# Attention in two chunks, and head work moved off GpSimd, in a decoder step on one core

## What is computed

```python
def step(carry, inp):                      # chunks of tokens, in order
    C, n, m = carry
    qc, kc, vc, li, lf = inp
    bcum = jnp.cumsum(lf, axis=-1)
    D = bcum[..., :, None] - bcum[..., None, :] + li[..., None, :]
    D = jnp.where(causal, D, -jnp.inf)
    inter = bcum + m[..., None]
    m_t = jnp.maximum(inter, jnp.max(D, axis=-1))
    s = jnp.einsum('bhjd,bhsd->bhjs', qc, kc) * jnp.exp(D - m_t[..., None])
    num = (jnp.einsum('bhjs,bhsd->bhjd', s, vc)
           + jnp.exp(inter - m_t)[..., None] * jnp.einsum('bhvk,bhjk->bhjv', C, qc))
    nq = jnp.sum(s, axis=-1) + jnp.exp(inter - m_t) * jnp.einsum('bhk,bhjk->bhj', n, qc)
    h = num / jnp.maximum(jnp.abs(nq), jnp.exp(-m_t))[..., None]
    w_s, decay = jnp.exp(bcum[..., -1:] - bcum + li - m_new[..., None]), ...
    C_new = decay[..., None, None] * C + jnp.einsum('bhs,bhsv,bhsk->bhvk', w_s, vc, kc)
```

## Time and profile before

| | us |
|---|---|
| median of three runs | 942.03 |
| lowest and highest | 940.66, 942.45 |
| span of the profiled execution | 940.7 |

### The profile page before, as it was taken

The page is one execution under the profiler, slowest core; times in us unless marked ns, Lnnn a source line. Parts: engine busy times, 40 slices in busy tenths (PEclk is TensorE's granted clock), DMA queues, the critical chain, the costliest instruction groups (busy, mean ns, idle before and its releaser), DMA issues. The chain is left out here.

```text
span 940.7 us, 18449 instructions
## 1 busy us (share of the span) xinstructions
PE 928.3 (99%) x6833; PEld 907.8 (96%) x6833; DVE 772.2 (82%) x1231; ACT 464.4 (49%) x684; POOL 106.7 (11%) x110
## 2 busy tenths in 40 slices
PE   8999999999999999999999999999999999999996
PEld 8999999999999999999999999999999999999995
DVE  6899985988698869876455569999888999889997
ACT  6654452445336324634833345456545555455664
POOL 3011330042006001500231000000000000000001
PEclk9999999999999999999999999999999999999998
DMA  6245216211620352042342222233222223232122
GB/s 219 68 150 198 69 57 224 90 45 56 246 90 23 134 191 90 23 150 87 117 140 68 89 73 84 90 108 106 102 90 91 90 68 113 90 116 109 46 91 100
DMA packets 22460, 98.56 MB, mean 105 GB/s; under 512 B 2929, under 2 KB 5122, under 8 KB 17909
## 3 DMA queue, kind: packets, MB, share of 16 engines
q1 hardware_dynamic: 19576, 77.13, 24.9%
q0 software_dynamic: 1984, 19.72, 5.7%
q10 hardware_dynamic: 832, 0.88, 0.3%
HBM read 85.28 MB, written 12.44 MB: 104 GB/s over the span
## 5 line engine op out<-in xcount | busy, mean ns | idle before, releaser
L1301 PE MATMUL ps<-h_hi,w_hi 128*128 128x288 f32 x896 | 193.7, 298 | 0.0
L1301 PE MATMUL ps<-h_lo,w_hi 128*128 128x288 f32 x896 | 191.7, 295 | 0.0
L1301 PE MATMUL ps<-h_hi,w_lo 128*128 128x288 f32 x896 | 191.4, 295 | 0.0
L793 ACT ACTIVATE w_hi<-raw 128x1024 fp32r<-128x1024 f32 x76 | 80.4, 1058 | 177.4 <-PE ps L1301 174.2
L1301 PEld LDWEIGHTS ps<-h_hi,w_hi 128*128 128x128 f32 x896 | 143.5, 189 | 1.3 <-issue 0.6
L1301 PEld LDWEIGHTS ps<-h_hi,w_lo 128*128 128x128 f32 x896 | 144.3, 189 | 0.0
L1301 PEld LDWEIGHTS ps<-h_lo,w_hi 128*128 128x128 f32 x896 | 144.2, 188 | 0.0
L1692 DVE TENSOR_TENSOR w_lo<-raw,w_hi 128x1024 fp32r<-128x1024 f32 x76 | 94.2, 1240 | 48.9 <-ACT w_hi L793 48.8
L1917 DVE SCALAR_TENSOR_TENSOR conv<-a_p,vec,conv x120 | 97.6, 813 | 0.2
L1569 PE MATMUL ps<-cols_b,late 128*128 128x288 f32 x432 | 62.8, 295 | 0.1
L1569 PE MATMUL ps<-cols_a,main 128*128 128x288 f32 x432 | 62.9, 295 | 0.0
(11 more groups left out here) (362 smaller groups left out, 1857.3 us busy)
## 6 DMA issues: line engine op xcount, KB each, us to landing
raw<-w_head_in SPq DMA_DIRECT2D x40, 512.0 KB, 3.5
raw<-w_fp_in SPq DMA_DIRECT2D x18, 1024.0 KB, 4.9
cs<-st_c_in POOLq DMA_DIRECT2D x4, 2048.0 KB, 9.6
c_s_out<-cs POOLq DMA_DIRECT2D x4, 2048.0 KB, 7.7
raw<-w_fo_in SPq DMA_DIRECT2D x8, 1024.0 KB, 4.9
x<-xT_in SPq DMA_DIRECT2D x16, 288.0 KB, 4.1
raw<-w_cgcv_in SPq DMA_DIRECT2D x8, 512.0 KB, 3.6
raw<-w_ga_in SPq DMA_DIRECT2D x8, 512.0 KB, 3.5
```

The source lines that it names most:

```text
L793: act.activation(w_hi[:, s, :], raw[:, s, :], ACT.Copy).then_inc(hi_ready, 1)
L1301: last = pe.matmul(ps[:, 2 * s + b, 0:HALF], wt[:, w, k * P:k * P + P], src[:, k, b * HALF:b * HALF + HALF], start=(k == 0 and wt is w_hi ...
```

## The change

S and PV are computed in two chunks of 256 prompt tokens. S0 and S1 end at column 256 (`S_END`). For the second chunk PV adds the weighted queries (`qt`, split into `qt_hi` by ACT and `qt_lo` by DVE) times the middle state (`cm32`, split into `cm_hi` and `cm_lo`). The middle state comes from four products between N and unit 7, evacuated by ACT; CP keeps the four products of the second chunk, and DVE, no longer ACT, adds the decayed middle state to it (`cp`). The exponentials per head go from eleven to nine.

The samples' stack is no longer placed by matmuls: DVE writes the high and low parts to `kvs`, and SP copies them with six transfers per head to `stk`, behind the load of unit 9's weights.

POOL's arithmetic in the heads goes: `cs_lo` to DVE (`old_lo`, eight of 512 columns), `wvs` to ACT (eight copies of 256 columns, scaled by a mask column). ACT makes unit 7's gate (`og_unit(7)`) with the high part for unit 9 behind the PV evacuations, and the first three `old_hi` ahead of unit 5's evacuation.

The convolution's 31 prompt taps become two chains, even taps into `conv`, odd ones into `kvn`, added at the end (`taps_end`). The samples' taps become, for each half of the samples, one product of 32 x 31 = 992 columns and one sum. All of this stands before DVE's products with S.

In the opening, the decays and item rows for the middle state are computed, and the placement matrices aren't. The core of the diff:

```diff
@@ -79,22 +79,28 @@
...
-S_USE, T_USE, I_USE, K_USE, PV_USE, CP_USE, CS_USE, N_USE, HT_USE = 0, 5, 10, 11, 13, 18, 20, 28, 29
+S_USE, T_USE, I_USE, CM_USE, PV_USE, CP_USE, CS_USE, N_USE, HT_USE = 0, 5, 10, 11, 13, 18, 20, 28, 29
...
-READER = ["dve"] * 5 + ["act"] * (5 + 1 + 2 + 5 + 2) + ["dve"] * (8 + 1 + 3)
+READER = ["dve"] * 5 + ["act"] * (5 + 1 + 2 + 5) + ["dve"] * (2 + 8 + 1 + 3)
-W_OFF = [0, 512, 896, 1152, 1280]
-W_COLS = 1280 + TS
+S_END = [TP // 2, TP // 2, TP, TP]
+W_OFF = [0, 256, 384, 640, 768]
+W_COLS = 768 + TS
+W_EXPS = [2, 3, 5, 6, 7]
+N_W = 7 + CHUNK
+N_PV = 4
...
 
-POOL_SET = 16
-DVE_HEAD_STEPS = 89
-CONV_TAPS = (4, 5, 5, 5, 4, 4, 2, 2, 0, 0)
+POOL_SET = 15
+DVE_HEAD_STEPS = 64
+CONV_TAPS = (5, 5, 6, 6, 5, 4, 0, 0, 0, 0)
...
             loads(U_A, w_cgcv, N_A, first=2)
-            loads(U_B, w_head, NH * PER_HEAD)
+            with sp.Fori(0, NH) as h:
+                for j in range(PER_HEAD):
+                    sp.wait_ge(lo_ready, h * PER_HEAD + (U_B + j - 1))
+                    sp.dma_start(raw[:, j % 2, :], w_head[bass.ds(h * PER_HEAD + j, 1)].rearrange("o p n -> (o p) n"))\
+                      .then_inc(raw_loaded[j % 2], 16)
+                sp.wait_ge(kvsplit_ready, h * 2 + 2)
+                for g in range(2):
+                    for r, src in enumerate(stacked):
+                        sp.dma_start(stk[r * GT:r * GT + GT, g, :].rearrange("p (c v) -> p c v", c=2).bitcast(F32),
+                                     src[g * GT:g * GT + GT, :, :].bitcast(F32)).then_inc(stk_placed[g], 16)
             loads(U_GA, w_ga, KT)
 
...
             def states(h, last=False):
 
-                for b in range(SB):
-                    pool.wait_ge(cshi_ready, h * SB + (b + 1))
-                    pool.tensor_tensor(cs_lo[:, b % RING, :], cs[:, b, :, :].rearrange("p k v -> p (k v)"),
-                                       cs_hi[:, b % RING, :].bitcast(F32), ALU.subtract).then_inc(cslo_ready, 1)
-
-                for g in range(2):
-                    pool.wait_ge(act_read, h * ACT_USES + (START + READER[:K_USE + g].count("act") + 1))
-                    pool.tensor_tensor(wvs[0:3 * GT, g * SG:g * SG + SG, :],
-                                       stk[0:3 * GT, g, HD:2 * HD].bitcast(F32).unsqueeze(1)
-                                       .broadcast_to([3 * GT, SG, HD]),
-                                       oh96[0:3 * GT, :].unsqueeze(2).broadcast_to([3 * GT, SG, HD]), ALU.mult)\
-                        .then_inc(wvs_ready, 1)
-
-                pool.wait_ge(act_read, h * ACT_USES + (START + ACT_USES))
+                pool.wait_ge(dve_read, h * DVE_USES + (START + 7))
                 pool.dma_start(cn_p[bass.ds(h, 1)].rearrange("o p k v -> (o p) k v"), cp[:, :, :])\
                     .then_inc(cp_stored, 16)
 
@@ -915,27 +941,31 @@
...
-                    for t in range(s + 1, NB):
+                    for t in range(s + 1, S_END[s] // P):
...
+                for t in range(CHUNK):
+                    at = (CHUNK + t) * P
+                    act.activation(wq[:, t * P:t * P + P], negm[:, bass.ds(h, 1), at:at + P]
+                                   .rearrange("p o n -> p (o n)"), ACT.Exp,
+                                   bias=dec[:, bass.ds(h, 1), D_Q + t:D_Q + t + 1].rearrange("p o n -> p (o n)"))\
+                        .then_inc(w_ready, 1)
...
+                hi_of(4)
+                evac_bias(h, 4, halves(qkv[:, 2, :, :], 0))
 
                 act.wait_ge(cs_loaded, h * 16 + 16)
                 for b in range(RING):
                     old_hi(b)
+                hi_of(5)
+                evac_bias(h, 5, halves(qkv[:, 2, :, :], 1))
+
+                act.wait_ge(qt_ready, h + 1)
+                act.activation(qt_hi[:, :, :], qt[:, :, :], ACT.Copy).then_inc(pvhi_ready, 1)
...
-                for g in range(2):
-                    use(K_USE + g)
-                    act.activation(stk[0:3 * GT, g, :], bank(K_USE + g)[0:3 * GT, :], ACT.Copy).then_inc(act_read, 1)
+
+                for k in range(2):
+                    use(CM_USE + k)
+                    act.activation(cm32[:, k, 0:VE], bank(CM_USE + k)[:, 0:VE], ACT.Copy).then_inc(act_read, 1)
...
+                act.wait_ge(act_read, h * ACT_USES + (START + 8))
+                act.activation(cm_hi[:, :, :], cm32[:, :, :], ACT.Copy).then_inc(pvhi_ready, 1)
                 act.wait_ge(out_stored, 16 * 4)
-                for j in range(6, 8):
-                    hi_of(j)
-                    act.wait_ge(unit_done, h * PER_HEAD + (U_B + j + 1))
-                    act.activation(halves(merged, h * 2 + (j - 6)), slot(j % 2), ACT.Sigmoid,
-                                   bias=vcol(h * PER_HEAD + (U_B + j))).then_inc(slot_read[j % 2], 1)
+                og_unit(6)
+
+                for b in range(SB):
+                    if b % SG == 0:
+                        act.wait_ge(stk_placed[b // SG], h * 48 + 48)
+                    act.activation(wvs[b // SG][0:3 * GT, b % SG, :], stk[0:3 * GT, b // SG, HD:2 * HD].bitcast(F32),
+                                   ACT.Copy, scale=oh96[0:3 * GT, b % SG:b % SG + 1]).then_inc(wvs_ready, 1)
                 for i in range(5):
                     use(PV_USE + i)
                     n = P if i < NB else TS
                     act.activation(num[0:n, i, :], bank(PV_USE + i)[0:n, 0:VE], ACT.Copy).then_inc(act_read, 1)
-                act.wait_ge(cp_free, h + START)
-                for k in range(2):
-                    use(CP_USE + k)
-                    act.activation(cp[:, k, :], bank(CP_USE + k)[:, 0:VE], ACT.Copy).then_inc(act_read, 1)
+                og_unit(7)
@@ -1392,7 +1424,7 @@
...
+                    t0, n, rows_ = (s * P, S_END[s] - s * P, P) if s < NB else (TP, TS, TS)
                     for k in range(2):
...
-                pe.wait_ge(place_ready, 4)
-                pe.wait_ge(kvsplit_ready, h * 2 + 2)
-                for g in range(2):
-                    use(K_USE + g)
-                    for c, (of_hi, of_lo) in enumerate(((2, 0), (1, 3))):
-                        for first, src in ((of_hi, kv_hi), (of_lo, kv_lo)):
-                            last = pe.matmul(bank(K_USE + g)[0:3 * GT, c * HD:c * HD + HD],
-                                             place3[0:TS, g, first:first + 3, :].rearrange("p r t -> p (r t)"),
-                                             src[0:TS, c * HD:c * HD + HD], start=(src is kv_hi), stop=(src is kv_lo))
+
+                pe.wait_ge(wv_ready, h * NB + CHUNK)
+                for k in range(2):
+                    use(CM_USE + k)
+                    for s in range(CHUNK):
+                        last = pe.matmul(bank(CM_USE + k)[:, 0:VE], kvn[:, s, k * P:k * P + P], wvn[:, s, :],
+                                         start=(s == 0), stop=(s == CHUNK - 1))
                     last.then_inc(attn_ready, 1)
                 head_unit(7)
...
-                        for s in range(t + 1):
+                        for s in range(t - t % CHUNK, t + 1):
...
+                        for k in range(2 if t >= CHUNK else 0):
+                            at = (t - CHUNK) * P
+                            for q_, c_ in ((qt_hi, cm_hi), (qt_hi, cm_lo), (qt_lo, cm_hi)):
+                                last = pe.matmul(bank(PV_USE + t)[:, 0:VE + 1], q_[:, k, at:at + P], c_[:, k, :],
+                                                 start=False, stop=(k == 1 and q_ is qt_lo))
...
-                    for s in range(NB):
+                    for s in range(CHUNK, NB):
...
-                pe.wait_ge(wvs_ready, h * 2 + 2)
+                for g in range(2):
+                    pe.wait_ge(stk_placed[g], h * 48 + 48)
+                pe.wait_ge(wvs_ready, h * SB + SB)
@@ -1904,17 +1947,46 @@
...
+                    o = (row(conv, h)[:, 0:TP], kvn[:, 0, 0:TP])[w % 2]
+                    a = row(a_p, h)[:, w:w + TP]
...
+                    else:
+                        steps.settle(back=1)
+                        steps.on(dve.scalar_tensor_tensor(o, a, wcol, o, ALU.mult, ALU.add))
+
+                def taps_end():
+                    o = row(conv, h)[:, 0:TP]
+                    steps.settle()
+                    steps.on(dve.tensor_tensor(o, o, kvn[:, 0, 0:TP], ALU.add))
+
+                def sample_taps(half):
+
+                    n = SB // 2
+                    rows_ = a_s[:, bass.ds(h, 1), half * n:half * n + n, 0:SL]
+                    dims = [list(d) for d in rows_.ap]
+                    shifted = bass.AP(rows_.tensor, rows_.offset, [dims[0], dims[2], dims[3], [dims[3][0], CW]])
+                    all_taps = vec[:, bass.ds(h * CW + V_WDW, CW)].unsqueeze(1).unsqueeze(1).broadcast_to([P, n, SL, CW])
+                    terms = num[:, 0:4, :].rearrange("p a n -> p (a n)")[:, 0:n * SL * CW]
+                    steps.on(dve.tensor_tensor(terms.rearrange("p (b j w) -> p b j w", b=n, j=SL), shifted, all_taps,
+                                               ALU.mult))
```

(93 more changed lines are left out.)

117 lines of the change are left out of this document (63 added, 54 removed).

## The result

The changed kernel takes 999.38 us (997.88 to 1002.41, 4 runs) where the kernel before takes 941.36 (940.66 to 942.45, 4 runs): a ratio of 1.062, between 1.0606 and 1.0634. Forecast were 995.5 us and a range from 963 to 1013. The profiled execution has a span of 1000.9 us, 60.2 more than that of before.

The account below looks back on a forecast made before the run. PE's work in the heads, plus any wait put before a matmul, bounds the kernel: -2.82 + 8.75 + 3.85 = +9.78 us a head gives 981.1; 14.4 for the clock gives 995.5 us, range 963 to 1013.

Parts of the forecast that it names:

- PE's work: PE's matmul time in the heads falls by 2.82 us a head, 11.3 us in four.
- First stall: PE stops before S3 until DVE has made S0's product: 8.75 us a head.
- rival (d): Wide strided sample products and sums cost DVE up to 7 us more than their columns: 1000 to 1024; chance 0.10.
- Gain by a silent POOL: Some 8 us of DVE time come back, all behind the S products, so priced at nothing.
- Stack by transfers: Six transfers a head on SP's queue land by 21 to 28, ACT wants them at 32: priced at nothing.
- Evacuations of PV: ACT's five PV evacuations follow eight stack products at 0.3 us net each; no PE wait for them in the sum.
- Second stall: In unit 8 PE waits before the third state update for DVE's first cp: 3.85 us a head, ends 0 and 5.5.
- Clock: Slower PE clock behind each stall costs 2.4 and 1.2 us a head, together 3.6, 14.4 in four heads.
- (a): Rival: both stalls occur but the clock stays up, 981.1 us; chance 0.13.
- (b): Rival: only the first stall, since ACT and DVE reach cp 4 us sooner than counted: 975.3 us; chance 0.12.
- (c): Rival: PE never waits and the time falls by its saved work, 930.7 us; chance 0.10.
- (e): Rival: a stall of just the 2.8 us saved, 942 us; chance 0.03.

Follow-up runs that it names:

- both undone: Changed kernel with DVE's S products moved ahead, unit 9's high part early and CP's banks read by ACT: 933.26 us, ratio 0.9912.
- S first: Changed kernel with DVE's products with S ahead of the sample taps, three old-state subtractions and unit 7's split: 957.04 us, ratio 1.0167.
- extra splits: Kernel before with two, four or seven added splits of unit 7's weights per head ahead of DVE's S products: 965.14, 980.43, 996.23 us.
- early high part: Changed kernel with ACT making unit 9's high part after the third PV evacuation, not the fifth: 985.42 us, ratio 1.048.
- cp by ACT: Changed kernel with ACT reading CP's banks, DVE adding the middle state later: 979.77 us with unit 9's high part early, 1003.79 us with it late.

## Why the prediction was right, point by point

By its own steps, with spans: +60.2 us = -11.6 (PE's work, by both undone) + 35.8 + 15.0 + 2.7 (waits) + 18.3 (the remainder, the clock). Forecast were -11.3 + 35.0 + 15.4 + 0 + 14.4.

**PE's work** (11.3): held, 11.6 by spans and 941.58 - 933.26 + 2.7 = 11.0 by medians.

**First stall** (8.75 us): 8.94. The chain of DVE's work was right link by link. From the end of unit 5 (208.51) the first half of the samples starts at -0.64 (forecast -0.6), S0's product at 10.81 (10.6). The open point, the sum over 992 columns, took 1.19 us, as long as the product ahead of it, which was the value taken; so the dear samples of rival (d) are excluded. The run with S first shows that this order and nothing else makes the wait.

**Gain by a silent POOL** (nothing): L1983's operation fell from 2.91 us to 1.23 and the 64x256 copy from 1.39 to 0.28, and DVE has nothing to show for it in the time, since it lies behind the S products. That held for the step from before to after. As a statement about the part alone it doesn't hold: with ACT's changed order and S first, POOL's subtractions hold up taps ahead of S and cost 24.5 us when given back. In the changed kernel's own DVE order this wasn't run. I looked for POOL only where it stood in the kernel before, and not where the changed order of ACT would let it start. The same oversight made the extra splits' expectations miss.

**Stack by transfers** (nothing):

```profile
stk<-kvs SPq DMA_DIRECT2D x24, 64.0 KB, 2.0
```

Nobody waits for them: held.

**Evacuations of PV** (no wait for them in the sum): wrong by 0.67 us a head. ACT's eight scaled copies take 3.30 us where I had taken 0.3 net for each; so they end up to 0.9 us later, and the first PV bank comes free late. That is the 2.7 us of the third wait. I had allowed for copies at their full durations, but only as the upper end of the second stall.

**Second stall** (3.85 us): 3.74, for the reason given: high part behind the PV evacuations, split, row statistics, cp. The early high part takes 2.0 us of it, and cp by ACT the rest once the high part is early. What cp by ACT gives with the high part unmoved stays open, since that run also moved the high part by 1.9 us. The upper end of 5.5 for slow copies doesn't follow from the rows: ACT's copies did take longer, and it still idled for 1.33 us before the fourth PV evacuation, waiting for PE, so that longer copies don't put the high part later behind PE's PV.

**Clock** (2.4 and 1.2 us a head): the direction held, the second size was too low. With only the first long wait in S left, the remainder is 978.5 - 940.7 + 11.6 - 35.7 - 2.7 = 11.0, 2.75 a head. With only the second it is 953.9 - 940.7 + 11.6 - 15.0 - 2.7 = 7.1, 1.8 a head, not 1.2; together 18.1, and the changed kernel shows 18.3. The direct count in the changed kernel gives the same 18.3, but 9.3 behind the first waits and 9.0 behind the second, 2.3 a head each. By the medians the remainders are 10.8, 8.8 and, for the changed kernel, 999.38 - 941.36 + 11.0 - 53.5 = 15.5: the profiled execution is the slowest of its four, 1002.41 us. So the whole term lies between 15.5 and 18.3 against 14.4, and the second price between 1.8 and 2.3 a head; how the whole splits between the two waits isn't fixed better than that, since single heads range from 1.6 to 3.3. I had taken the middle between nothing and the first price; the extra splits show 1.8 for a wait of the same length. The rows near the end of before were the better guide: there too the clock had fallen after less. The Trainium skill (TensorE: Matmul & The Clock Gate, What's actually happening) has the throttled state as the default that activity releases; the rows behind both waits agree, and a sum without the clock would have missed 15 to 18 us.

**Rivals.** (a), the clock stays up, is refuted by the stages, and (b), no second stall, by the waits. (c), faster by 11.3 us, is what the kernel becomes with both causes undone: it needed DVE's product 8.75 us earlier. Here another order gave it; less work in the same order wasn't run. (e) is refuted by the size of the wait.

So the forecast was 3.9 us too low. By spans it is 60.2 - 53.5 = 6.7: 3.9 of clock, 2.7 of the third wait, 0.4 of the two long ones, less 0.3 of extra saved work; the profiled execution stands 3.0 us above its median, and the sum was made against the median of before, so 2.9 us of the 6.7 don't appear between the medians (60.2 against 999.38 - 942.03 = 57.3).

## What to carry to other kernels

On an engine that is never idle, the price of a change isn't the busy time that it adds or takes away, but the point at which each of its waits is released: write the feeding engine's order out from the last point where it must wait, and put what nobody is waiting for behind the operation that somebody is. When one cause of a wait is removed, look for the next in the same order, and ask of each engine that starts earlier whom it will now run beside. Count a long wait of PE with what its clock costs behind it, here 1.6 to 3.3 us each.
